# Loads in order of use with two units computed chunk by chunk at the start, stick-breaking scores on both row halves, and new tables of order

## What is computed

```python
def stick_breaking(q, k, v):            # 8 heads of 64, 512 tokens, blocks of 128 queries
    def block(args):
        qi, i = args
        z = jnp.einsum('bhqd,bkhd->bhqk', qi, k).astype(jnp.float32) * scale
        qpos = i * SB_BLOCK + jnp.arange(SB_BLOCK)
        mask = kpos[None, :] < qpos[:, None]
        log_beta = jax.nn.log_sigmoid(z)
        log_1m = jnp.where(mask, jax.nn.log_sigmoid(-z), 0.0)
        suffix = lax.cumsum(log_1m, axis=3, reverse=True) - log_1m
        w = jnp.where(mask, jnp.exp(log_beta + suffix), 0.0)
        return jnp.einsum('bhqk,bkhd->bqhd', w.astype(v.dtype), v)
```

## Time and profile before

| | us |
|---|---|
| median of 3 runs | 1134.96 |
| lowest, highest of them | 1132.03, 1136.96 |
| the profiled execution | 1133.61 |
| its span in the profile | 1131.9 |
| mean granted clock of PE | 0.996 of full |

### The profile page before, as it was taken

How to read it: one execution, slowest core, us unless ns; L and a number is a source line. 1 busy time by engine, 2 the same in 40 slices (tenths; PEclk the granted TensorE clock), 3 DMA queues, 4 the chain that set the end, 5 groups by cost and what they waited for, 6 DMA issues and landing times.

```text
span 1131.9 us, 15155 instructions
## 1 busy us (share of the span) xinstructions
PE 1115.5 (99%) x5422; PEld 914.8 (81%) x5422; DVE 670.3 (59%) x881; ACT 491.7 (43%) x715; POOL 9.0 (1%) x26
## 2 busy tenths in 40 slices
PE   8999999999999999999999999999999999999996
PEld 7787777788888888888888887778888888888886
DVE  6446445855777777773334565656777776763234
ACT  5557465734444434442323455644344443432220
POOL 1000000000000000000000000000000000000000
PEclk9999999999999999999999999999999999999998
DMA  6221111232322223223334213122222222223332
GB/s 231 75 82 50 61 70 38 78 105 83 108 93 93 93 99 105 83 74 94 100 101 144 91 57 91 56 94 82 104 93 93 93 101 103 76 80 100 93 98 75
DMA packets 32777, 102.94 MB, mean 91 GB/s; under 512 B 3537, under 2 KB 5730, under 8 KB 32738
## 3 DMA queue, kind: packets, MB, share of 16 engines
q1 hardware_dynamic: 32002, 100.17, 27.0%
q10 hardware_dynamic: 736, 2.24, 0.6%
HBM read 99.84 MB, written 2.10 MB: 90 GB/s over the span
## 4 chain that ended last, share of the span: by engine, by line
PE 96%; DMA 1%; issue 1%; DVE 1%; ACT 0%; POOLq 0%; POOL 0%; ACTq 0%; DVEq 0%; SPq 0%
PE ps L1243 30%; PE ps L1245 29%; PE ps L1244 29%; PE ps L1443 2%; PE ps L1453 1%; PE ps L1471 1%; PE ps L1594 1%; PE ps L1568 1%; DMA v1s<-v 1%; PE ps L1578 1%; DMA x<-xT 1%; PE ps L1462 0%; PE ps L1522 0%; PE ps L1300 0%; PE ps L1531 0%
## 5 line engine op out<-in xcount | busy, mean ns | idle before, releaser
L1243 PE MATMUL ps<-h_hi,w_hi 128*128 128x512 f32 x888 | 351.3, 396 | 3.8 <-DVE h_lo L894 3.8
L1245 PE MATMUL ps<-h_hi,w_lo 128*128 128x512 f32 x888 | 346.3, 390 | 0.0
L1244 PE MATMUL ps<-h_lo,w_hi 128*128 128x512 f32 x888 | 346.2, 390 | 0.0
L609 ACT ACTIVATE w_hi<-w_raw 128x1024 fp32r<-128x1024 f32 (+2 forms) x146 | 139.0, 952 | 418.6 <-PE ps L1245 418.6
L876 DVE TENSOR_TENSOR w_lo<-w_raw,w_hi 128x1024 fp32r<-128x1024 f32 (+2 forms) x146 | 158.9, 1088 | 151.8 <-ACT w_hi L609 151.0
L1243 PEld LDWEIGHTS ps<-h_hi,w_hi 128*128 128x128 f32 x888 | 167.1, 188 | 41.2 <-issue 5.4
L1245 PEld LDWEIGHTS ps<-h_hi,w_lo 128*128 128x128 f32 x888 | 167.0, 188 | 35.4
L1244 PEld LDWEIGHTS ps<-h_lo,w_hi 128*128 128x128 f32 x888 | 167.2, 188 | 34.8 <-issue 1.2
L1243 PE MATMUL ps<-y_hi,w_hi 128*128 128x512 f32 x330 | 128.4, 389 | 0.0
L1244 PE MATMUL ps<-y_lo,w_hi 128*128 128x512 f32 x330 | 128.4, 389 | 0.0
L1245 PE MATMUL ps<-y_hi,w_lo 128*128 128x512 f32 x330 | 128.4, 389 | 0.0
(11 more groups left out here) (225 smaller groups left out, 1241.2 us busy)
## 6 DMA issues: line engine op xcount, KB each, us to landing
w_raw<-w_up SPq DMA_DIRECT2D x88, 512.0 KB, 3.2
w_raw<-w_mix SPq DMA_DIRECT2D x53, 512.0 KB, 3.2
w_raw<-w_down SPq DMA_DIRECT2D x32, 384.0 KB, 3.1
w_raw<-w_down SPq DMA_DIRECT2D x32, 320.0 KB, 2.9
out<-x SPq DMA_DIRECT2D x8, 256.0 KB, 2.2
x<-xT SPq DMA_DIRECT2D x2, 512.0 KB, 8.1
x<-xT ACTq DMA_DIRECT2D x2, 512.0 KB, 8.1
bias_sb<-bias ACTq DMA_DIRECT2D x1, 512.0 KB, 4.1
```

Of the source, the lines that this page charges most:

```text
L609: s.activation(w_hi[r % SPL][:, 0:cols], w_raw[r][:, 0:cols], ACT.Copy).then_inc(w_hi_ready, 1)
L1243: mm(dst, w[0], m[0], start=first, stop=False, skip_group_check=shared)
L1244: mm(dst, w[0], m[1], start=False, stop=False, skip_group_check=shared)
L1245: return mm(dst, w[1], m[0], start=False, stop=last, skip_group_check=shared)
```

## The change

Three things. (1) The start: x comes in eight transfers of one chunk, units 0 and 1 in two halves of four chunks each, issued in the order of their use; of the parameters only the norm gains come first, the rest after the last `h_hi`. ACT and DVE split units 0 and 1 by halves. PE does unit 0 chunk c, then unit 1 chunk c, for c = 0 to 7. (2) For heads 1 to 7 the score matmuls of 384 and 128 columns read copies of q and k in the other partition half (`q_swap`, `k_swap`, which are `sq` and `ssq`). SP makes these copies by four DMAs of 64 x 512 for each head pair, once the pair's keys are evacuated and the scores of the pair before are done. They stand in SP's list between the unit loads, which no longer are a loop. The clearing of `ssq` after the first norm moves to behind head 7's `z_soft`. (3) Both tables are new.

```diff
+def swap_before(j):
+    steps = [(name, i) for name, i, _ in SEQ0]
+    before = steps[:steps.index(("z", 2 * j - 1))] if j else []
+    running = max([i for name, i in before if name == "unit"], default=0)
+    return max(running, MIX0.index(("kb", j))) + RAW + 1
...
-    fill = q[:4] + k[:4] + q[4:] + k[4:] + parts_of(range(2, N0))
+    fill = sum((q[c:c + 1] + k[c:c + 1] for c in range(KC)), []) + parts_of(range(2, N0))
...
-            for u in range(RAW):
+            load_half(sp, 0, 0)
+            load_half(sp, 1, 0)
+            for c in (2, 3):
+                load_x(sp, c)
+            load_half(sp, 0, 1)
+            load_x(sp, 4)
+            load_half(sp, 1, 1)
+            for c in (5, 6, 7):
+                load_x(sp, c)
+            for u in (2, 3):
                 sp.dma_start(w_raw[u][:, :], w_mix0[u]).then_inc(w_loaded[u], 16)
...
+            def swap_halves(j):
+                sp.wait_ge(a_taken, a_before(MIX0, MIX0.index(("kb", j))) + 1)
+                if j:
+                    sp.wait_ge(sb_z, 2 * j)
+                for dst, t in ((q_swap, qbT), (k_swap, kbT)):
+                    for half in range(2):
+                        sp.dma_start(dst[SD * (1 - half):SD * (2 - half), :],
+                                     t[SD * half:SD * half + SD, j, :]).then_inc(sb_swapped, 16)
...
+                    if i >= FIRST_SWAPPED:
+                        pe.wait_ge(sb_swapped, 64 * (j + 1))
+                    other = slice(SD * (1 - i % 2), SD * (2 - i % 2))
                     for b in (0, 1, 3, 2):
-                        mm(zs[:, ZOFF[b]:ZOFF[b] + ZW[b]], kbT[rows, j, b * P:(b + 1) * P],
-                           qbT[rows, j, b * P:T], start=b != 3, stop=False, skip_group_check=True)
+                        kT, qT = kbT[rows, j, :], qbT[rows, j, :]
+                        if i >= FIRST_SWAPPED and b in (1, 3):
+                            kT, qT = k_swap[other, :], q_swap[other, :]
+                        mm(zs[:, ZOFF[b]:ZOFF[b] + ZW[b]], kT[:, b * P:(b + 1) * P], qT[:, b * P:T],
+                           start=b != 3, stop=False, skip_group_check=True)
...
-EVENTS1 = ((2, "split", 2), (6, "ssq", 0), (10, "rinv", 0), (10, "split", 3), (21, "split", 4), (26, "s", 0),
+EVENTS1 = ((7, "split", 2), (7, "ssq", 0), (10, "split", 3), (16, "split", 4), (16, "rinv", 0), (26, "split", 5),
```

More of the change, by code:

```diff
@@ L330, in trunk @@
         b_half = sem("b_half")
-        x_loaded = [sem(f"x_loaded{i}") for i in range(4)]
+        x_loaded = [sem(f"x_loaded{c}") for c in range(KC)]
+        gains_loaded = sem("gains_loaded")
+        half_loaded = [sem(f"half_loaded{u}") for u in range(2)]
+        half_hi_ready = sem("half_hi_ready")
+        half_lo_ready = sem("half_lo_ready")
         par_loaded = sem("par_loaded")
@@ L349, in trunk @@
         b_taken = sem("b_taken")
+        sb_swapped = sem("sb_swapped")
         sb_z = sem("sb_z")
@@ L516, in one @@
                 return t[bass.ds(i, 1)].rearrange("o p c -> (o p) c")
-            for u in range(RAW):
+            load_half(sp, 0, 0)
[8 more added lines that the diff above has]
+            for u in (2, 3):
                 sp.dma_start(w_raw[u][:, :], w_mix0[u]).then_inc(w_loaded[u], 16)
-                if u < 2:
-                    i = 3 * u
-                    sp.dma_start(x[:, 2 * i:2 * i + 2, :], x_pair(i)).then_inc(x_loaded[i], 16)
             sp.dma_start(wg2_sb[:, :], wg2).then_inc(wg2_loaded, 16)
[L524 to L527, removed]
+            def swap_halves(j):
[6 more added lines that the diff above has]
+                                     t[SD * half:SD * half + SD, j, :]).then_inc(sb_swapped, 16)
+            for u in range(RAW, U_UP0):
+                for j in range(SH // 2):
+                    if u == swap_before(j):
+                        swap_halves(j)
                 unit(u, u % RAW, w_mix0[u])
@@ L628, in rinv_copy, with half_hi @@
                 s.activation(rinv[:, :], ps[:, B_RINV, :], ACT.Copy).then_inc(rinv_ready, 1)
-            act.dma_start(par[:, :], small).then_inc(par_loaded, 16)
-            for i in (1, 2):
-                act.dma_start(x[:, 2 * i:2 * i + 2, :], x_pair(i)).then_inc(x_loaded[i], 16)
+            act.dma_start(par[:, 0:S_CONV], small[:, 0:S_CONV]).then_inc(gains_loaded, 16)
+            load_x(act, 0)
+            load_x(act, 1)
+            def half_hi(u, half):
+                act.wait_ge(w_loaded[u] if half else half_loaded[u], 16)
+                s.activation(w_hi[u][:, W_HALVES[half]], w_raw[u][:, W_HALVES[half]],
+                             ACT.Copy).then_inc(w_hi_ready if half else half_hi_ready, 1)
             for c in range(KC):
-                if c % 4 == 0:
-                    act.wait_ge(w_loaded[c // 4], 16)
-                    s.activation(w_hi[c // 4][:, :], w_raw[c // 4][:, :], ACT.Copy).then_inc(w_hi_ready, 1)
+                if c % 4 < 2:
+                    half_hi(c % 4, c // 4)
                 if c == 0:
-                    act.wait_ge(par_loaded, 16)
-                if c % 2 == 0:
-                    act.wait_ge(x_loaded[c // 2], 16)
+                    act.wait_ge(gains_loaded, 16)
+                act.wait_ge(x_loaded[c], 16)
                 s.activation(h_hi[:, c, :], x[:, c, :], ACT.Copy, scale=gain_at(0, c)).then_inc(hi_ready, 1)
+            act.dma_start(par[:, S_CONV:S_END], small[:, S_CONV:S_END]).then_inc(par_loaded, 16)
             def b_evac(dst, n_cols, src, tiles):
```

78 lines of the change are left out of this document (46 added, 32 removed), and 6 rows, old and new, of the table EVENTS1.

## The result

| | us |
|---|---|
| changed kernel, median of 4 runs | 1123.51 (1123.03 to 1125.07) |
| before, median of 4 runs beside it | 1135.76 (1132.03 to 1136.96) |
| ratio, with its 95% interval | 0.9913 (0.9896 to 0.9929) |
| the profiled executions: before, changed | 1133.61, 1123.61 |
| their spans | 1131.9, 1121.8 |

The forecast was 1123.3. The total is right; of its four terms the scores are right to 0.1 us, the gate transposes to 0.2, and the start and layer 1 are off by 1.5 and 0.5. Two profiled executions are compared here, and they differ by 10.0 us. The table gives the terms; where a stretch is named by matmuls, it is the start times of matmuls of `three`, counted from the first of the program.

What follows compares the result with a forecast made beforehand. PE was taken as the bound, with 96% of the chain of waits. Terms -3.8 - 5.9 + 0.4 - 1.8 = -11.1 us from a level of 1134.4 gave 1123.3 us, range 1120.0 to 1127.5.

Steps and rivals of the forecast that it cites:

- What bounds: Whole kernel: PE is 96% of the chain of waits, so time is won only on PE.
- Scores: Layer 0, heads 1 to 7: row halves run side by side, eight records take 1.51 us, 0.84 less a head; -5.9 us.
- The copies: Layer 0, q and k copies for each head pair: they land in time; 0 us, with 0.3 in the range.
- the slower rival: Layer 0: a pair's four copies land one after another, 13.6 us in all, scores wait, clock falls; 1139.4 us, chance 0.03.
- Start: Up to matmul 48: x lands some 2.5 us earlier, PE starts at 6.95 without a clock drop; -3.8 us.
- the second rival: Start: small transfers cost more than their bytes, PE starts at 7.8 or later at 1.2 GHz; 1125.3 us, chance 0.12.
- Thin margins: Squares and layer 0 heads 1 and 6: margins 0.7 to 1 us, charged nothing; rival of waits 1126.3 us, chance 0.15.
- Gate transposes: Layer 0: two of three eighths ahead of them are gone, so PE waits; +0.4 us.
- Layer 1: New order: 2.3 of the 2.5 us wait for shifted values goes, transposes 4 lose 0.8; net -1.8 us.
- Sum: Whole kernel: the terms give -11.1 us against a level of 1134.4, forecast 1123.3 us.

Runs made afterwards that it cites:

- the two moved splits: Changed kernel with layer 1's table of before, in which splits 11 and 12 moved behind the copy of the values: median 1124.40 us, ratio 0.9918.
- the mixed heads: Changed kernel with another assignment to row halves or issue order of the four score matmuls in heads 2 to 7: 1123.93 us, one run.
- the kernel where it began at 7.33: Changed kernel with x chunk 0 first on ACT's queue, and the first half unit, then the gains, first on SP's: 1124.23 us, one run.

## Why the prediction was right, step by step

**What bounds.** Right: PE has 96% of the chain in both kernels, and the gain is the sum of what changed on PE.

**Scores, -5.9.** Right in size and in reason. 1.51 us were worked out for halves of 768 and 512 columns, 1.49 were measured, and the mixed heads showed that the longer half counts.

**The copies, 0.** The number was right, its bounds were not. Here each lands in 2.3 us:

```profile
sq<-qbT SPq DMA_DIRECT2D x8, 128.0 KB, 2.3
```

I had bounded it by the 6.8 us of the shift of the values, and the slower rival was built on that row. The 6.8 were the price of company, as the two moved splits showed; no other transfer moved in the microseconds ahead of any of the four sets of copies. But they can be late for another reason, the place of the keys in DVE's list, which with the old table cost 1.7 us.

**Start, -3.8.** Too much by 1.5. The step that failed is the path of the first chunk: "which stand first in their queues; with what is under way beside them that is at most 0.8 MB, so x lands some 2.5 us earlier". On ACT's queue the norm gains stand ahead of x, and on SP's queue the transfers behind the first half unit were under way beside both. x landed at 6.83, and by then 1.3 MB had moved (0.98 MB by 6 us, the sum over the stretches from 1 us on, and 383 GB/s behind it). So PE began at 8.57, later than the 7.8 by which I had bounded it: the first half of the second rival came true, its low clock did not. (The late end of that term, 1.8, should by its own numbers have been 9.40 - 7.8 = 1.6.) With x at the head of one queue and the half unit and then the gains on the other, `h_hi` started at 5.22. The rate was lower as well, 0.24 to 0.28 MB/us from 3 to 6 us and not 0.39; at the rates of before 0.98 MB would have been through near 5.2. The page DMA: Bandwidth & Descriptors of the Trainium skill, section Bandwidth, advises to batch transfers to 1 MiB or more. I set it aside because the trace had its rate with 512 KB; with 256 KB the rate was lower up to 8 us, at 399 GB/s or more behind that. That is the direction of the page's rule, but no run here separates the size of the transfers from the 176-byte rows of the gains, which moved in the same microseconds, and the order alone brought the first chunk in time at the low rate.

Of the measured 2.3, about 1.1 is the start's own, by the kernel with the old start at full clock (matmul 48 at 20.48); 1.2 is the low clock of the one execution of before. That split rests on single executions: in the seven with the changed start and 14 constant matmuls, matmul 48 started between 19.07 and 20.07. The cause I gave for the gain in clock ("with 0.2 us of idle time I expect no drop") did not hold: PE was idle for 2.25 us, and the clock stayed. Nor is 6.81 the floor of the first product, as I had it: the constant matmuls ended between 6.32 and 7.65, by when the clock rose. The page TensorE: Matmul & The Clock Gate of the Trainium skill, part 1, says that the number of matmuls at the low clock differs between runs of one kernel. The traces agree: of the 27 steps between the 28 constant records of the changed kernel, 15 were at the low pace in one profiled execution and all 27 in the other.

**Thin margins, 0.** The number was right. No suffix step waits. At the squares the margin of 0.7 was luck: DVE finished them at 22.65 and not at 21.3, since it was through with the last `h_lo` at 14.9 and not at 13.5 and had three short operations on constants next that I had left out. PE asked for the squares only at 23.66 because it had begun late. Had it asked at 22.0, as forecast, it would have waited 0.6 us; in the kernel where it began at 7.33, it waited 0.4.

**Gate transposes, +0.4.** 0.24 measured, and it is gone in the kernel where they stand one eighth later.

**Layer 1, -1.8.** 2.3 measured. The wait at transposes 4 is 0.3 instead of 0.8. Put on one time base (the products just ahead of it stand 7.9 us apart in the two traces), ACT ended the copy some 0.4 us sooner than I had it, and PE asked for it a little later. Of the wait for the values I saw the order but not its cause: I let `o 0` come later by 2.1 us and kept the 6.8 us of the transfer, and what happened is that the transfer took 3.2.

**Sum.** The terms gave 11.1 against a level of 1134.4. The profiled executions differ by 10.0 and that of before stood at 1133.6, so the two errors, 1.1 too much gain and 0.8 too high a level, nearly cancelled. That part was luck: the forecast was closer than its steps deserved. That the median beside the result moved by 12.25 is the level of four runs of before; the ratios of both groups say 10 us with 2 either way. Undone one at a time, the scores give 6.0 to 6.5, the start 2.0 to 2.5 and layer 1's table 3.5 us, each with 2.5 to 3.5 of uncertainty; their sum, about 12, agrees with the whole within that.

## What to carry to other kernels

The time of one transfer in a trace belongs to its company, so before it is used as a price, look at what the other queues moved in that stretch; here a split on ACT and DVE started the load that slowed a transfer on which PE waited. For the first product, put the things it needs at the heads of the queues, and count small transfers as well: the last of the three sets the start. Matmuls with a contraction of 64 cost here what the longer row half costs, in each of the four orders of issue that were tried, so the copies that make the other half usable pay as soon as they can land unseen. A margin that holds because the step ahead came late is no margin.

## What the hardware showed that I had not expected

- Two row halves run past each other in the list: a matmul behind four records of the other half started 0.01 us after the first of them.
- The two transfers of the same shift of 448 KB took 4.7 to 7.2 us beside unit loads (four kernels) and 2.7 to 4.3 without or almost without them.
- The kernel before has runs from 1131.7 to 1138.2 us, and their mean granted clock goes with the time: at 0.997 they took 1131.7 to 1133.2, at 0.993 1135.8 to 1136.9. A wait of PE cost more than its length in some executions: behind the wait of 2.8 us the clock fell in both profiled executions that had it with the new start, and behind the wait at the FFN norm of layer 1, 1.2 to 1.4 us, in 5 of the 14 profiled executions, for about 1.6 us each. Once it fell at 84.2 us, behind a wait of 0.2. The ten runs of the changed kernel, which has fewer waits, lie within 2.4 us; that the waits are the reason is not shown.
- The first product of the changed start came at 8.26 to 9.29 us in eight profiled executions. Whatever gains less than 1 us there can't be read from one trace.
